# A decoder layer on one core: the front before the expert gathers rewritten

## The reference

```
proj = x @ w_in  -> q, k, v, iq, ik, iw, z, xbc, dt
attn = sparse attention, 8 heads x 64: an indexer (iq, ik, iw) scores all causal keys,
       the 64 best of each query are attended (rope on q, k, iq, ik)
ssd  = Mamba-2 scan, 8 heads x 64, chunk 128: causal conv of 4 taps and SiLU on xbc,
       decay from dt, gate silu(z), grouped RMS norm
h    = LayerNorm(alpha * x + concat(attn, ssd) @ w_out)
PEER: per token and head (8): q = h @ wq -> two halves; s1 = q1 @ k1.T, s2 = q2 @ k2.T (128 keys each)
      16 best of each side, their 256 sums, 16 best of these -> 16 expert numbers and softmax gates
      act = gelu(h . u[expert]) * gate;  ffn = sum over experts of act * v[expert]
out  = LayerNorm(alpha * h + ffn)
```

## Time and profile before

| | |
|---|---|
| median of 3 runs | 810.52 us (810.42 to 813.33) |
| profiled execution | 812.53 us, its span 810.8 us |
| TensorE clock granted, mean of the span | 0.836 of full speed, 1.00 in every stretch used below |
| busy: TensorE, VectorE, ScalarE, GpSimd | 69%, 68%, 55%, 35% |
| moved by DMA | 301 MB, 371 GB/s over the span |

### The profile page before, as it was taken

How to read it: one execution, slowest core, us unless ns; L and a number is a source line. 1 busy time by engine, 2 the same in 40 slices (tenths; PEclk the granted TensorE clock), 3 DMA queues, 4 the chain that set the end, 5 groups by cost and what they waited for, 6 DMA issues and landing times.

```text
span 810.8 us, 10116 instructions
## 1 busy us (share of the span) xinstructions
PE 555.7 (69%) x3343; PEld 462.3 (57%) x3343; DVE 547.8 (68%) x1388; ACT 449.4 (55%) x805; POOL 283.2 (35%) x267
## 2 busy tenths in 40 slices
PE   6999999998967879665545455608554645554695
PEld 4476487775857878564545454607554644454642
DVE  3388487798764667676767676299767676676554
ACT  1035146769744667565656565519665656565532
POOL 0000002545723435434334444306644434444400
PEclk9999999999988989867787867658777677777689
DMA  8991015999999999999999999998999999999992
GB/s 294 386 384 58 0 53 207 370 424 420 421 419 420 421 422 420 421 422 421 420 422 421 422 420 422 422 422 350 422 422 422 422 422 420 422 421 424 422 420 114
DMA packets 51353, 301.08 MB, mean 371 GB/s; under 512 B 5576, under 2 KB 7920, under 8 KB 17520
## 3 DMA queue, kind: packets, MB, share of 16 engines
q0 software_dynamic: 36864, 268.45, 80.1%
q1 hardware_dynamic: 13232, 31.92, 10.6%
q10 hardware_dynamic: 1216, 0.19, 0.1%
HBM read 299.49 MB, written 1.05 MB: 371 GB/s over the span
## 4 chain that ended last, share of the span: by engine, by line
DMA 45%; DVE 22%; PE 18%; issue 6%; ACT 4%; POOL 3%; SPq 0%; DVEq 0%; POOLq 0%; ACTq 0%
DMA arena<-in_expert_uv,expert 44%; DVE arena L1479 6%; PE bank L487 5%; PE bank L637 5%; PE bank L657 3%; POOL arena L458 3%; PE bank L602 2%; ACT arena L998 2%; ACT weight L988 1%; DMA arena<-in_w_idx 1%; PE bank L618 1%; DVE score L1458 1%; DVE score L1456 1%; DVE picked L1459 1%; DVE big L1239 1%
## 5 line engine op out<-in xcount | busy, mean ns | idle before, releaser
L637 PE MATMUL bank<-ident,arena 128*128 128x128 f32 x1920 | 304.0, 330 | 231.9 <-ACT arena L998 231.9
L458 POOL DMA_INDIRECT arena<-in_expert_uv,expert x256 | 281.6, 1100 | 485.2 <-PE bank L637 265.9
L637 PEld LDWEIGHTS bank<-ident,arena 128*128 128x128 f32 x1920 | 281.6, 174 | 256.3 <-ACT arena L998 254.0
L1479 DVE SCALAR_TENSOR_TENSOR arena<-x_sb,arena 128x1024 f32<-128x1024 f32 x256 | 307.2, 1224 | 178.0 <-DMA arena<-in_expert_uv,expert 178.0
L998 ACT ACTIVATE arena<-arena,weight 128x1024 f32<-128x1024 f32 x240 | 257.0, 1138 | 2.2
L983 ACT ACTIVATE gelu<-dots 128x4 f32<-128x4 f32 (+2 forms) x76 | 15.5, 204 | 224.8 <-DVE arena L1479 224.2
L487 PE MATMUL bank<-arena,x_t 128*128 128x512 f32 (+1 forms) x128 | 54.7, 580 | 6.2 <-DMA arena<-in_w_idx 6.2
L988 ACT ACTIVATE weight<-gelu,gate 128x1 f32<-128x1 f32 x256 | 55.9, 285 | 3.5
L487 PEld LDWEIGHTS bank<-arena,x_t 128*128 128x128 f32 x128 | 24.9, 203 | 29.6 <-issue 25.7
L618 PE MATMUL bank<-x_t,arena 128*128 128x128 f32 x256 | 29.9, 276 | 0.0
L657 PE MATMUL bank<-arena,mid 128*128 128x512 f32 x64 | 29.3, 622 | 0.0
(11 more groups left out here) (206 smaller groups left out, 499.7 us busy)
## 6 DMA issues: line engine op xcount, KB each, us to landing
arena<-in_w_in SPq DMA_DIRECT2D x5, 2048.0 KB, 19.8
arena<-in_w_out SPq DMA_DIRECT2D x2, 2048.0 KB, 18.3
arena<-in_expert_uv,expert POOLq DMA_INDIRECT x256, 25.9
arena<-in_peer_wq SPq DMA_DIRECT2D x4, 1024.0 KB, 10.2
mix<-in_peer_wq SPq DMA_DIRECT2D x2, 1024.0 KB, 7.1
big<-in_peer_wq SPq DMA_DIRECT2D x2, 1024.0 KB, 8.2
arena<-in_w_idx SPq DMA_DIRECT2D x4, 304.0 KB, 6.7
x_t<-in_x_columns SPq DMA_DIRECT2D x4, 256.0 KB, 5.9
```

The source lines that it names most:

```text
L458: pool.indirect_dma_start(out=arena[:, slot * SLOT:(slot + 1) * SLOT], out_offset=None, in_=expert_uv, in_offset=bass.IndirectOffsetOnAxis ...
L637: last = mm(banks[2 * tile + k // 4][:, (k % 4) * P:(k % 4 + 1) * P], lhsT=arena[:, at + k * P:at + (k + 1) * P], rhs=ident[:, :], is_tran ...
L1479: ins = stt(rows, x_rows[:, bass.ds(tile * D_MODEL, D_MODEL)], 1.0, rows, ALU.mult, ALU.mult, accum_out=dots[:, parity, j:j + 1])
```

## The change

- The index weights (four transfers) are issued by ScalarE, ahead of its small loads, and no longer by SyncE between those of x's columns.
- Keys and conv taps come transposed from memory straight to `keys_t` and `conv_t`. Job `consts` and VectorE's two copies out of it go.
- Two of z's eight k-steps of tile 0 are multiplied before cb, four after attention, two after y.
- Half of tile 1's logits come behind the transposes of h. In `queries`, each half of h is waited for by itself; the first head's first side has a bank of its own (`first_q`), is copied out and scored (`first_scores`) apart, with the state matmuls (`carry_state`) between the two sides' scores. VectorE searches both sides in PSUM.
- Both xbc projections of tile 1 come before the transposed probabilities.
- `route_first_pairs` names the eight best experts of the first head, takes tile 1's row maximum, then names the other eight. GpSimd waits for `first_experts`, and before the ninth gather for `experts_ready`. ScalarE takes the state and the first xbc copy before the exponentials, and the second before the probabilities.

The diff, cut to its core (both key arrays and the taps are transposed on the way in):

```diff
-    jobs = [("proj_idx", t) for t in both] + [("proj_q", t) for t in both] + [("T_idx", t) for t in both] + [("consts",)]
+    jobs = [("proj_idx", t) for t in both] + [("proj_q", t) for t in both] + [("T_idx", t) for t in both]
     jobs += [("proj_k", 0)] + idx_dots[0] + [("proj_k", 1), ("T_qk", 0, 0), ("T_qk", 1, 0)] + idx_dots[1] + sums[0] + logits[0]
-    jobs += [("proj_xbc", 0, 0), ("proj_xbc", 0, 1)] + probs[0] + [("proj_v", 0), ("cb", 0), ("T_xs", 0), ("pv", 0), ("proj_z", 0)]
+    jobs += [("proj_xbc", 0, 0), ("proj_xbc", 0, 1)] + probs[0] + [("proj_v", 0), ("proj_z", 0), ("cb", 0), ("T_xs", 0), ("pv", 0)]
     jobs += [("T_attn", 0), ("y_diag", 0), ("out", 0, 0), ("T_y", 0), ("out", 0, 1)]
-    jobs += [("T_qk", 0, 1), ("T_qk", 1, 1), ("T_b",)] + sums[1] + logits[1] + [("T_h", 0, 0), ("T_h", 0, 1), ("state",)]
-    jobs += [("peer_q", 0, 0), ("key_scores", 0, 0), ("proj_xbc", 1, 0)] + probs[1] + [("proj_xbc", 1, 1), ("proj_z", 1), ("peer_q", 0, 1)]
+    jobs += [("T_qk", 0, 1), ("T_qk", 1, 1), ("T_b",)] + sums[1] + logits[1][0:2] + [("T_h", 0, 0), ("T_h", 0, 1)] + logits[1][2:4]
+    jobs += [("first_q",), ("peer_q", 0, 0), ("first_scores",), ("state",), ("key_scores", 0, 0), ("proj_xbc", 1, 0), ("proj_xbc", 1, 1)] + probs[1] + [("proj_z", 1), ("peer_q", 0, 1)]
     jobs += [("key_scores", 0, 1), ("proj_v", 1), ("pv", 1), ("cb", 1), ("T_xs", 1), ("y_off",), ("T_attn", 1), ("y_diag", 1), ("peer_q", 0, 2)]
     jobs += [("key_scores", 0, 2), ("out", 1, 0), ("out", 1, 1), ("T_y", 1), ("peer_q", 0, 3), ("key_scores", 0, 3)]
...
             for part in range(4):
                 ks = slice(2 * part, 2 * part + 2)
                 sp.dma_start(x_t[:, ks, :], x_columns.rearrange("(k p) n -> p k n", p=P)[:, ks, :]).then_inc(idx_in[part], 16)
-                sp.dma_start(chunk(places["idx"], IDX_COLS + SSD_HEADS)[:, ks, :],
-                             w_idx.rearrange("(k p) n -> p k n", p=P)[:, ks, :]).then_inc(idx_in[part], 16)
...
-            sp.wait_ge(keys_in, 4 * 16)
+            sp.wait_ge(keys_in, 3 * 16)
...
-                pool.wait_ge(experts_ready, u + 1)
+                if isinstance(u, int) and u == 0:
+                    pool.wait_ge(first_experts, 1)
+                else:
+                    pool.wait_ge(experts_ready, u + 1)
                 for j, slot in enumerate(slots_of(u)):
+                    if isinstance(u, int) and u == 0 and j == 8:
+                        pool.wait_ge(experts_ready, 1)
...
                 pe.wait_ge(w_in_sem[f"wq{h}"], 16)
-                pe.wait_ge(h_t_ready, 2 * (t + 1))
-                wait_bank(pe, job)
                 for n in range(2):
+                    job = ("first_q",) if (t, h, n) == (0, 0, 0) else ("peer_q", t, h)
+                    if n == 0 or (t, h) == (0, 0):
+                        wait_bank(pe, job)
                     for k in range(KT):
+                        if n == 0 and k % 4 == 0:
+                            pe.wait_ge(h_t_ready, 2 * t + k // 4 + 1)
                         last = mm(bank(job)[:, n * P:(n + 1) * P], lhsT=head_weights(h)[:, k, n * P:(n + 1) * P],
                                   rhs=h_t[:, k, t * P:(t + 1) * P], start=k == 0, stop=k == KT - 1)
+                    if n == 1 or (t, h) == (0, 0):
+                        last.then_inc(full(job), 1)
+            def carry_state():
+                job = ("state",)
+                pe.wait_ge(b_nat_ready, 1)
+                wait_bank(pe, job)
+                for g in range(GROUPS):
+                    heads = slice(g * GROUP_HEADS, (g + 1) * GROUP_HEADS)
+                    last = mm(bank(job)[:, g * 256:(g + 1) * 256], lhsT=b_nat[:, g, :],
+                              rhs=xdt_end[:, heads, :].rearrange("p a b -> p (a b)"), start=True, stop=True)
                 last.then_inc(full(job), 1)
             def scores_of_keys(t, h):
                 job = ("key_scores", t, h)
+                if (t, h) == (0, 0):
+                    job = ("first_scores",)
+                    pe.wait_ge(first_side_taken, 1)
+                    wait_bank(pe, job)
+                    mm(bank(job)[:, 0:P], lhsT=queries_of(0, 0)[:, 0, :], rhs=keys_t[:, 0, :], start=True, stop=True).then_inc(full(job), 1)
+                    carry_state()
+                job, sides = ("key_scores", t, h), range((t, h) == (0, 0), 2)
                 pe.wait_ge(peer_q_ready, query_order.index((t, h)) + 1)
                 wait_bank(pe, job)
-                for n in range(2):
+                for n in sides:
                     last = mm(bank(job)[:, n * P:(n + 1) * P], lhsT=queries_of(t, h)[:, n, :],
                               rhs=keys_t[:, n, :], start=True, stop=True)
...
-            job = ("consts",)
-            pe.wait_ge(keys_in, 4 * 16)
-            wait_bank(pe, job)
-            for s in range(2):
-                nc.tensor.transpose(bank(job)[:, s * P:(s + 1) * P], keys_nat[:, s, :], ident[:, :])
-            rows = (CONV_WIDTH + 1) * CT
-            nc.tensor.transpose(bank(job)[:, 2 * P:2 * P + rows], conv_nat[0:rows, :], ident[0:rows, 0:rows]).then_inc(full(job), 1)
+            pe.wait_ge(keys_in, 3 * 16)
...
+            pe.wait_ge(w_in_sem["z"], 16)
+            project(("proj_z", 0), "z", 0, ks=range(0, 2))
             pe.wait_ge(silu_ready, 2)
             cb_and_xs(0)
             attend(0)
-            pe.wait_ge(w_in_sem["z"], 16)
-            project(("proj_z", 0), "z", 0, ks=range(0, 5))
+            project(("proj_z", 0), "z", 0, ks=range(2, 6))
             transposed_attention(0)
             y_diagonal(0)
-            project(("proj_z", 0), "z", 0, ks=range(5, KT))
+            project(("proj_z", 0), "z", 0, ks=range(6, KT))
...
-            logits_of(1)
+            logits_of(1, range(0, 2))
             transposed_h(0, 0)
             transposed_h(0, 1)
-            job = ("state",)
-            pe.wait_ge(b_nat_ready, 1)
-            wait_bank(pe, job)
-            for g in range(GROUPS):
-                heads = slice(g * GROUP_HEADS, (g + 1) * GROUP_HEADS)
-                last = mm(bank(job)[:, g * 256:(g + 1) * 256], lhsT=b_nat[:, g, :],
-                          rhs=xdt_end[:, heads, :].rearrange("p a b -> p (a b)"), start=True, stop=True)
-            last.then_inc(full(job), 1)
+            logits_of(1, range(2, 4))
             queries(0, 0)
             scores_of_keys(0, 0)
             project_xbc(1, 0)
+            project_xbc(1, 1)
             transposed_probs(1)
-            project_xbc(1, 1)
...
         def _(act):
+            for part in range(4):
+                ks = slice(2 * part, 2 * part + 2)
+                act.dma_start(chunk(places["idx"], IDX_COLS + SSD_HEADS)[:, ks, :],
+                              w_idx.rearrange("(k p) n -> p k n", p=P)[:, ks, :]).then_inc(idx_in[part], 16)
             for t in range(TILES):
                 act.dma_start(pos_i[:, t:t + 1], positions[t * P:(t + 1) * P].rearrange("(p a) -> p a", a=1)).then_inc(angles_in, 16)
             act.dma_start(freqs, cast_rows(inv_freq)).then_inc(angles_in, 16)
             for n, source in enumerate((dt_bias, a_log, d_skip)):
                 act.dma_start(heads_in[:, n * SSD_HEADS:(n + 1) * SSD_HEADS], cast_rows(source)).then_inc(heads_vec_in, 16)
-            act.dma_start(keys_nat[:, 0, :], peer_k1).then_inc(keys_in, 16)
-            act.dma_start(keys_nat[:, 1, :], peer_k2).then_inc(keys_in, 16)
-            act.dma_start(conv_nat[0:CONV_WIDTH * CT, :], conv_w.rearrange("k (c p) -> (k c) p", p=P)).then_inc(keys_in, 16)
-            act.dma_start(conv_nat[CONV_WIDTH * CT:(CONV_WIDTH + 1) * CT, :], conv_b.rearrange("(c p) -> c p", p=P)).then_inc(keys_in, 16)
+            for s, source in enumerate((peer_k1, peer_k2)):
+                act.dma_start(keys_t[:, s, :], source).then_inc(keys_in, 16)
+            act.dma_start(conv_t[:, :], conv_taps).then_inc(keys_in, 16)
...
-            take_state()
-            take_queries(0, 0)
-            take_scores(0, 0)
-            exp_logits(1)
+            job = ("first_q",)
+            wait_job(act, job)
+            run(queries_of(0, 0)[:, 0, :], bank(job)[:, 0:P], ACT.Copy).then_inc(free(job), 1)
+            act.wait_ge(free(job), use(job))
+            act.sem_inc(first_side_taken, 1)
+            job = ("peer_q", 0, 0)
+            wait_job(act, job)
+            run(queries_of(0, 0)[:, 1, :], bank(job)[:, P:2 * P], ACT.Copy).then_inc(free(job), 1)
+            act.wait_ge(free(job), use(job))
+            act.sem_inc(peer_q_ready, 1)
             wait_job(act, ("out", 0, 1))
             exp_decay(1)
+            take_state()
+            take_xbc(1, 0)
+            exp_logits(1)
             exp_gate(act, 0)
-            take_xbc(1, 0)
+            take_xbc(1, 1)
             take_probs(1)
-            take_xbc(1, 1)
...
+                if t == 0:
+                    take_row_max(0)
+            def take_row_max(t):
+                nk = (t + 1) * P
...
-            job = ("consts",)
-            wait_job(dve, job)
```

(40 more changed lines are left out.)

39 lines of the change are left out of this document (24 added, 15 removed).

## The result

| | before | after |
|---|---|---|
| median, range of the runs | 811.31 us (810.42 to 815.02, 5 runs) | 806.46 us (805.57 to 807.17, 5 runs) |
| ratio after to before, 95% interval | | 0.992 (0.9898 to 0.9941) |
| profiled execution, its span | 812.53 us, 810.8 us | 807.17 us, 805.4 us |

The kernel is faster by 0.8%, the whole interval beyond the 0.5% that I had set as the least to be told; the forecast was 0.40%. Beside three of its variants it ran again: 807.25 us (806.52 to 807.38, 5 runs), ratio 0.9915 (0.9885 to 0.9944). The time lies within 0.9 us of the forecast 807.3. The gain is twice the forecast one, and I had given a gain beyond 0.5% a chance of only 0.32. Between the two profiled executions 5.4 us are gone, where I had summed 3.26.

The account below looks back on a forecast made before the run. Bound: GpSimd's expert gathers, nearly 640 of 810.8 us at 420 GB/s, starting without holes when tile 1's z projection ends. Terms 0.5 + 0.5 + 1.76 + 0.5 = 3.26 off 810.5 gave 807.3 us; 8-in-10 range 804.6 to 810.4.

Parts of the forecast that it names:

- the 420 GB/s: DMA rate of the expert gather stream from the ninth page slice on; claimed to stand unchanged.
- Three transposes: TensorE before the k projection: keys and taps loaded transposed take 0.5 us off the path (0.3 to 0.5).
- z's two k-steps: Tile 0's z projection: two k-steps moved into TensorE's 1.94 us hole before cb, worth 1.76 us, low bound 0.9.
- Small loads and k weights behind the index weights: Front queues: small loads some 3 us later, k weights about 2 us later, at cost 0.
- The late softmax: Second tile's exponentials end at 130.3, TensorE wants them at 131.0: cost 0, slack 0.7; chance 0.08 of being slower.
- the hole behind gather four: DMA stream between gathers four and five: a hole that was hardly there before would appear.
- The signs that I had named as wrong: TensorE idle before transposed probabilities, early first gather with fifth unmoved, or not 367 GB/s in 20 us after the fifth.
- The arrival of q: Front: index weights on ScalarE's queue bring the q weights 0.5 us sooner, bounds 0 and 1.4.
- From layer norm to xbc: TensorE from h's transposes to the second xbc projection: 7.0 instead of 7.49 us, gain 0.5, bounds 0 and 0.87.
- the end of z(1) on TensorE: End of the second tile's z projection, 140.15 us before; claimed to free the fifth gather's slot and set the kernel's end.
- the early naming: First head's routing: first eight experts named early, first gather 3.5 us sooner; worth 0 in time, upper bound 0.7.
- early gathers and feeding count: Rival: hole-free stream starts with the first gathers, or milder gains; 803.7 or 805.6 us, middle 805.2; chance 0.27.

Follow-up runs that it names:

- small_behind: Kernel before, all large loads in SyncE's queue as they were, ScalarE's small loads held until half the index data has landed: 811.57 us, one execution.
- z_before_probs_again: Second run of the changed kernel with tile 1's z projection ahead of the transposed probabilities, first rows scaled before probabilities are copied: 806.7 us, ratio 0.9911.
- hole_filled_with_nothing: Kernel before, with two useless k-steps (four matmul instructions, result overwritten) in TensorE's hole before cb: 812.0 us, ratio 0.9982.
- queue_only: Kernel before, with only the index weights moved to ScalarE's queue, ahead of its small loads: 811.24 us, ratio 0.9972.
- z_move_undone: Changed kernel with tile 0's z k-steps back where they were, none in TensorE's hole before cb: 811.72 us, ratio 0.9977.
- first_head_routed_as_before: Changed kernel with the old routing: row maximum first, one naming of 16 experts, sides still searched apart: 806.75 us, ratio 0.9914.
- z_move_only: Kernel before, with only tile 0's z k-steps placed as in the change: 809.19 us, ratio 0.9953.
- all_named_first: Changed kernel, but GpSimd waits for all 16 expert numbers, tile 1's row maximum still between the eights: 811.93 us, ratio 0.9973.

## Why the prediction came out as it did

**What was right.** The bytes and the 420 GB/s stand. Three transposes: 0.5 foretold, 2.31 - 1.81 = 0.50 measured. z's two k-steps: 1.76 foretold, 4.08 - 2.38 = 1.70 measured, and 1.69 alone on the kernel before. Small loads and k weights behind the index weights: free, though the delay was larger than I had put it; SyncE asks for the k weights at 16.87 instead of 12.53, 4.3 us later where I had said about 2. This leaves the DMA engines at 224 GB/s in 10 to 18, and k, v and z still come in time. The late softmax: free, and its cover as thin as foretold: the exponentials were done at 125.73, TensorE took up the probabilities at 126.37, 0.64 of slack where I had 0.7. The 2.7 us by which the first gather moved further than z(1) don't start the stream sooner: the hole behind gather four is there (57 GB/s), and the 18 us that begin 1.6 us behind gather five carry 365 GB/s, where I had said 367. The signs that I had named as wrong did not come, unless one counts the rate from gather five itself (336 against 358, the end of the hole).

**Terms that were mis-sized.** The arrival of q: 0.5 taken, 0 to 1.4 as bounds, 1.81 measured. I had costed it from the bytes that better feeding would bring, 4 x 50 KB by the rate of 4 to 5 us, which was itself a disturbed rate: 299 GB/s, where the changed kernel has 389. small_behind names the cause of most of it, loads of a few bytes a row ahead of the large ones: 1.3 of the 1.8. The Trainium skill (DMA: Bandwidth & Descriptors, section "Issuing engines are not separate DMA queues") would have the second issuer save only issue time. No run contradicts it: SyncE issued the last half of q's weights at 6.87 before, at 5.41 in small_behind and at 3.59 after, and the 0.3 to 0.6 us left to the second queue is smaller than what q's start varies by (0.9) from one execution to the next with one front. Where full, the engines gave the same to both: 385 before, 390 and 392 in the second and third slices after. From layer norm to xbc: 0.5 taken, 0.92 measured. My own terms (0.55 + 1.05 + 3.8 + 0.3 + 1.1 + 0.3) add up to 7.1 and not 7.0, so the gain should have read 0.4. What was smaller than put is the last part: from the start of the queries (107.09) to xbc pass 4.99 us, where I had put 5.5; the rows of state and scores start at 110.77, 110.99 and 111.86, closer together than their lengths put end to end. Together 1.31 + 0.42 = 1.73 more than summed: 3.26 + 1.73 = 4.99, which is TensorE's 5.00.

**The step that failed.** The sizes above explain the number; one step of the mechanism fell short as well: "So the end moves with **the end of z(1) on TensorE**", and from it the price of the early naming, "what it brings I put at **0**". The start of the stream has a second gate: the first two gathers' landing, dot products, GELU, scaling, and then TensorE's first sum. It ended 0.16 us behind z(1) in the kernel before. I had written that the first scaled row would be ready "still before z(1) ends", and had not looked up when it is in the trace. It was nearly right: in the changed kernel that row is ready by 135.01, when z(1) ends. But this holds only thanks to the early naming. With z(1) 5 us sooner and the gathers only as much sooner as VectorE's shorter path makes them, TensorE waits 2.07 us (old routing) or 4.62 us (all sixteen named first). The three kernels stand in a row: first gather at 120.29, 124.17, 126.56; idle before the first sum 0, 2.07, 4.62; tenth gather at 147.00, 149.31, 153.43. The early naming is what lets TensorE's 5.0 through to gather ten. Of its 2.3 us there against the old routing 1.0 is left at the last gather, and in the median none can be told: as a price in time, my 0 is not refuted by this pair. The 4.7 us stand against another order, in which the maximum stands between the eights and no gather starts before the sixteenth name. My rival "early gathers and feeding count" had the time nearly right (805.2) for another reason: the first gathers don't start the stream sooner, they feed TensorE's first sum, from which the way to gather ten is 11.98 or 11.99 us in nine of the kernels. (It is longer where TensorE waited again behind it, 12.91 in small_behind and 12.42 in z_before_probs_again, or had a lower clock.)

**The scale.** That 807.3 lies so near the measured 806.46 is partly luck. I took the forecast from a median of three, 810.52; beside the changed kernel the kernel before took 811.31, so the base was 0.8 us too low and the gain 1.6 too small (3.26 against 4.85), and the two errors cancel in part. Over 62 more executions the kernel before lies between 809.65 and 817.68, 46 of them at 812 to 816; the changed kernel's ten keep within 1.8 us. So the median gains more than the traces do: 814.35 - 807.25 = 7.1 beside the last variants, 5.4 between the traces. Without z in TensorE's hole the changed kernel scatters like that too. But hole_filled_with_nothing does as well, so at least one other source of the scatter is left in the kernel before, and no run here names it.

## What to carry to other kernels

When a stream starts on slots that several engines free, look up the instant of every chain that ends at the first reuse, not only of the one that ended last: here two were 0.16 us apart, and TensorE's chain moved alone stops at the other (2.07 us of idleness with the old routing). An idle gap of 2 us on TensorE costs its length and, in one profiled execution of four, 3.4 us more by the clock behind it; filling it with work that is needed anyway is worth trying first. When two traces are compared, shift the window with the event that it follows. A transfer rate read while loads of a few bytes are in flight is no ceiling for the large loads behind them.

## What the runs showed of the hardware

Small loads ahead of large ones: with positions, frequencies, keys and taps (some of them 4 bytes a row) issued first, 299 and 249 GB/s in 4 to 5 and 5 to 9 us; issued behind, 389 and 373 with two issuing engines, 258 and 344 with one. Over the whole of 2 to 9 us that is 230, 347 and 322 GB/s. The run with one issuing engine is a single execution.

The clock: after 1.93 or 1.94 us of idleness TensorE's granted clock was 0.66 and then 0.50 (1.2 GHz) in one profiled execution (queue_only) and stayed at 1.00 (2.4 GHz) in three others with the same gap (before, small_behind, z_move_undone) and after 2.07 us in first_head_routed_as_before; after 4.62 us it was 0.57. Matmul groups in such a stretch took 1.4 to 1.7 times as long (3.27 for 1.90, 6.52 for 4.51, 3.34 for 2.05). The Trainium skill (TensorE: Matmul & The Clock Gate, section "HAM oscillation — how this bites in real kernels") tells of idle gaps that bring the clock down; the traces agree that it can happen, and add that a gap of one length does it in some executions and not in others.

The landing of a gather: from the request of the second gather to the first use of its rows, where VectorE stood waiting for them, passed 7.4 to 8.6 us: 7.44 in z_move_only, 7.55 before, 7.58 in hole_filled_with_nothing, 7.77 in queue_only, 8.38 in small_behind, 8.39 in first_head_routed_as_before, 8.57 in all_named_first. In the last two the third gather was requested 1.3 us behind the second, in the others 4.2; small_behind shows that this spacing is not the whole reason. In the changed kernel VectorE used the rows 9.37 us after their request and waited for nothing, so it doesn't show when they landed.
